# A rotation of three weight buffers instead of two across the last two weight quads of a sparse layer and the first of the next

## The reference

```python
def hybrid_layer(x, norm_g, w_in, ..., w_branch, w_out):
    h = rmsnorm(x, norm_g)
    proj = h @ w_in
    ...
    for i, o in enumerate((o_nsa, o_pool, o_conv, o_fox)):
        branch = (o * jax.nn.silu(gates[:, :, i])) @ w_branch[i]
        term = jax.nn.sigmoid(merge[:, :, i]) * branch
        acc = term if acc is None else acc + term
    return x + acc @ w_out
```

## Time and profile before

| what | value |
|---|---|
| median of 3 runs | 2235.05 us (2233.2 to 2238.94) |
| profiled execution, own time | 2234.29 us |
| its span in the profile | 2231.6 us |
| PE busy | 2156.6 us, 97% |
| DVE, ACT, POOL busy | 51%, 45%, 36% |
| mean granted PE clock | 0.995 |
| DMA | 189.32 MB, mean 85 GB/s |

### The profile page before, as it was taken

The page is one execution under the profiler, slowest core; times in us unless marked ns, Lnnn a source line. Parts: engine busy times, 40 slices in busy tenths (PEclk is TensorE's granted clock), DMA queues, the critical chain, the costliest instruction groups (busy, mean ns, idle before and its releaser), DMA issues.

```text
span 2231.6 us, 31209 instructions
## 1 busy us (share of the span) xinstructions
PE 2156.6 (97%) x11281; PEld 1772.5 (79%) x11281; DVE 1132.0 (51%) x2003; ACT 1004.3 (45%) x1950; POOL 794.7 (36%) x347
## 2 busy tenths in 40 slices
PE   5999999999989999999999999999999999999998
PEld 4788888788887888888887887777777787777776
DVE  5799999565442457452436532222286623222374
ACT  5768787752343433222223434444633434444631
POOL 2511111444464134444443333332343433333342
PEclk9999999999999999999999999999999999999998
DMA  3212111423333122223322222222223222222221
GB/s 142 91 57 63 64 61 62 142 85 97 101 124 95 39 76 85 95 94 95 103 94 100 89 77 71 67 76 67 85 93 120 87 83 75 69 67 68 85 95 57
DMA packets 51732, 189.32 MB, mean 85 GB/s; under 512 B 6564, under 2 KB 7204, under 8 KB 51108
## 3 DMA queue, kind: packets, MB, share of 16 engines
q1 hardware_dynamic: 48096, 175.13, 24.4%
q10 hardware_dynamic: 2452, 6.88, 0.8%
q0 software_dynamic: 1072, 5.77, 0.7%
HBM read 185.66 MB, written 2.10 MB: 84 GB/s over the span
## 4 chain that ended last, share of the span: by engine, by line
PE 78%; DVE 10%; ACT 4%; DVEq 3%; issue 2%; POOL 2%; DMA 0%; ACTq 0%; POOLq 0%
PE bank L350 21%; PE bank L352 20%; PE bank L351 20%; PE bank L951 2%; PE bank L994 2%; POOL weight_lo L382 1%; PE bank L977 1%; DVE wide_region L2264 1%; ACT wide_region L1078 1%; DVE wide_region L2267 1%; ACT weight_hi L376 1%; PE bank L425 1%; PE bank L609 1%; PE bank L915 1%; PE bank L830 1%
## 5 line engine op out<-in xcount | busy, mean ns | idle before, releaser
L382 POOL TENSOR_TENSOR weight_lo<-weight_slots,weight_hi 128x1024 fp32r<-128x1024 f32 x277 | 676.4, 2442 | 1020.5 <-ACT weight_hi L376 1015.1
L376 ACT ACTIVATE weight_hi<-weight_slots 128x1024 fp32r<-128x1024 f32 x272 | 288.0, 1059 | 778.5 <-PE bank L352 694.3
L350 PE MATMUL bank<-h_hi,weight_hi 128*128 128x512 f32 x1144 | 461.5, 403 | 2.3 <-issue 1.0
L351 PE MATMUL bank<-h_lo,weight_hi 128*128 128x512 f32 x1144 | 446.1, 390 | 0.0
L352 PE MATMUL bank<-h_hi,weight_lo 128*128 128x512 f32 x1136 | 443.5, 390 | 0.0
L350 PEld LDWEIGHTS bank<-h_hi,weight_hi 128*128 128x128 f32 x1144 | 214.8, 188 | 49.8 <-issue 3.1
L352 PEld LDWEIGHTS bank<-h_hi,weight_lo 128*128 128x128 f32 x1136 | 213.2, 188 | 45.8
L351 PEld LDWEIGHTS bank<-h_lo,weight_hi 128*128 128x128 f32 x1144 | 215.2, 188 | 40.5 <-issue 0.5
L382 POOL TENSOR_TENSOR head_weight_lo<-weight_slots,head_weight_hi 128x1024 fp32r<-128x1024 f32 x28 | 67.3, 2406 | 280.4 <-DVE v_region L1728 133.0
L350 PE MATMUL bank<-h_hi,head_weight_hi 128*128 128x512 f32 x336 | 139.2, 414 | 5.4 <-DVE h_lo L399 2.8
L2233 DVE RECIPROCAL small<-small 128x1 f32<-128x1 f32 x128 | 20.5, 160 | 230.2 <-ACT attention_work L1521 230.2
(11 more groups left out here) (491 smaller groups left out, 4484.4 us busy)
## 6 DMA issues: line engine op xcount, KB each, us to landing
weight_slots<-weights SPq DMA_DIRECT2D x328, 512.0 KB, 3.4
wide_region<-cmp_w ACTq DMA_DIRECT2D x2, 2048.0 KB, 8.6
v_region<-ssm_bc POOLq DMA_DIRECT2D x8, 256.0 KB, 4.4
residual<-x_in POOLq DMA_DIRECT2D x1, 2048.0 KB, 9.0
out<-normed SPq DMA_DIRECT2D x4, 512.0 KB, 2.7
residual<-x_in SPq DMA_DIRECT2D x2, 512.0 KB, 5.1
residual<-x_in ACTq DMA_DIRECT2D x2, 512.0 KB, 9.8
v_region<-mem_in POOLq DMA_DIRECT2D x1, 1024.0 KB, 5.1
```

Of the source, the lines that this page charges most:

```text
L350: pe.matmul(to, w_h[:, k, :], hi[:, k, 0:width], start=(k == 0), stop=False)
L351: pe.matmul(to, w_h[:, k, :], lo[:, k, 0:width], start=False, stop=False)
L376: act.activation(parts[0][s % 2], slot[s], ACT.Copy).then_inc(w_hi[s], 1)
L382: eng.tensor_tensor(parts[1][at], slot[s], parts[0][at].bitcast(F32), ALU.subtract).then_inc(w_lo[s], 1)
```

## The change

The buffers main 0, side, main 1 are used in turn for 12 blocks: those of quads `q0 + 17` and `q0 + 18` and, behind layer 0, those of the first quad of layer 1 (`W_TURN`). The text numbers these blocks n = 0 to 11. Block n may now be split when PE has finished block n - 3. Layer 1's last two quads take part as well, without a next layer. The loop over `ob` now splits blocks n = 1, 0 and 2 at its last two turns, n = 1 without any wait for PE; POOL takes n = 1 before n = 0 too. The first quad of sparse layer 0 stays as it was.

```diff
+        W_TURN = [[[W_MAIN[n][0], W_NEXT[n][1], W_MAIN[n][1]][(4 * q + i) % 3] for i in range(4)]
+                  for q in range(3) for n in range(2)]
+        W_TURN = [W_TURN[2 * q:2 * q + 2] for q in range(3)]
...
+                parts = W_TURN[2] if L else W_NEXT
...
-                both(pe, q0 + 17, ACC_HI, ACC_LO, SL * L + (S_L2 + S_ACC))
+                for i in range(2):
+                    for s in range(4):
+                        gemm(pe, q0 + 17 + i, s, ACC_HI, ACC_LO, T, SL * L + (S_L2 + S_ACC) if i + s == 0 else None,
+                             parts=W_TURN[i])
...
+            def turn_weight_hi(quad, n):
+
+                s, last = n % 4, n - 3
+                act.wait_ge(w_full[s], 16 * (quad + n // 4) + 16)
+                if last >= 0:
+                    act.wait_ge(mm_done[last % 4], quad + last // 4 + 1)
+                elif s != 1:
+                    act.wait_ge(mm_done[2 if s == 0 else 3], quad)
+                act.activation(W_TURN[n // 4][0][s], slot[s], ACT.Copy).then_inc(w_hi[s], 1)
...
-                next_weight_hi(q0, 3)
+                if L == 0:
+                    next_weight_hi(q0, 3)
+                else:
+                    turn_weight_hi(q0 - 2, 11)
...
                 for ob in range(KT + 1):
-                    if ob < KT:
+                    if ob < KT - 2:
                         ahead(act, q0 + (15 + ob // 4), ob % 4)
+                    elif ob == KT - 2:
+                        turn_weight_hi(q0 + 17, 1)
+                        turn_weight_hi(q0 + 17, 0)
+                    elif ob == KT - 1:
+                        turn_weight_hi(q0 + 17, 2)
                     if ob:
                         round_hi(act, stages + S_ACC, ob - 1, ACC_HI[:, ob - 1, :], ACC[:, ob - 1, :])
                 act.wait_ge(ms_ready, L + 8)
                 for blk in range(KT):
                     s, quad = blk % 4, q0 + (17 + blk // 4)
-                    if blk < KT - 2:
-                        ahead(act, quad, s)
-                    elif blk == KT - 1 and L + 1 < LAYERS:
-                        next_weight_hi(q0 + QL, 1)
-                        next_weight_hi(q0 + QL, 0)
+                    if blk + 3 < KT or L + 1 < LAYERS:
+                        turn_weight_hi(q0 + 17, blk + 3)
...
-                if L + 1 < LAYERS:
-                    next_weight_hi(q0 + QL, 2)
...
-                with pool.Fori(0, QL - 1) as i:
+                with pool.Fori(0, QL - 3) as i:
                     quad = pool.snap(i + (q0 + 1))
                     for s in range(4):
                         weight_lo(pool, quad, s)
+                for s in (1, 0, 2, 3):
+                    weight_lo(pool, q0 + 17, s, W_TURN[0])
+                for s in range(4):
+                    weight_lo(pool, q0 + 18, s, W_TURN[1])
```

More of the change, by code:

```diff
@@ L826, in _, with scaled_terms @@
             idle_products(pe, 18)
-            def scaled_terms(s, k):
-                w_h, w_l = W_NEXT[0][s], W_NEXT[1][s]
+            def scaled_terms(s, k, parts):
+                w_h, w_l = parts[0][s], parts[1][s]
                 pe.matmul(bank[s][:, :], w_h[:, k, :], T_HI[:, k, :], start=(k == 0), stop=False)
@@ L846, in _ @@
                         for s in range(2):
-                            scaled_terms(s, k)
+                            scaled_terms(s, k, parts)
                         pe.wait_ge(sq_ready, 7 * KT + (k + 1))
@@ L856, in _ @@
                             norm_sums(pe, L + 7, L + 6)
-                        scaled_terms(0, k)
+                        scaled_terms(0, k, parts)
                     pe.wait_ge(w_lo[1], q0 + 1)
@@ L861, in _ @@
                             norm_spread(pe, L + 7)
-                        scaled_terms(1, k)
+                        scaled_terms(1, k, parts)
                 pe.wait_ge(w_lo[2], q0 + 1)
@@ L866, in _ @@
                         norm_spread(pe, L + 7)
-                    scaled_terms(2, k)
+                    scaled_terms(2, k, parts)
                 pe.wait_ge(w_lo[3], q0 + 1)
                 for k in range(KT):
-                    scaled_terms(3, k)
+                    scaled_terms(3, k, parts)
                 if L:
@@ L2397, in _ @@
                 q0 = QL * L + Q_L2
-                weight_lo(pool, q0, 1, W_NEXT)
-                weight_lo(pool, q0, 0, W_NEXT)
                 if L == 0:
+                    weight_lo(pool, q0, 1, W_NEXT)
+                    weight_lo(pool, q0, 0, W_NEXT)
                     norm_power(pool, 6)
                     pool.wait_ge(rstd_ready, 7)
-                weight_lo(pool, q0, 2, W_NEXT)
+                    weight_lo(pool, q0, 2, W_NEXT)
+                else:
+                    for s in range(3):
+                        weight_lo(pool, q0, s, W_TURN[2])
                 norm_power(pool, L + 7)
                 pool.wait_ge(rstd_ready, L + 8)
-                weight_lo(pool, q0, 3, W_NEXT)
-                with pool.Fori(0, QL - 1) as i:
+                weight_lo(pool, q0, 3, W_TURN[2] if L else W_NEXT)
+                with pool.Fori(0, QL - 3) as i:
                     quad = pool.snap(i + (q0 + 1))
```

## The result

The changed kernel takes 2244.81 us (median of 7 runs, 2242.2 to 2246.47), the kernel before 2236.92 us beside it (7 runs). The ratio is 1.0036 with an interval of 1.0025 to 1.0047: slower by some 8 us. The forecast of 2241.9 us for a change of +6.8 us had the sign and most of the size. The prediction gave 0.49 each to slower and to the same by a line of 0.3%; the measured 0.36% lies just above it, so that it fell on the slower side of that line is not something the prediction foresaw. The profiled execution took 2244.25 us, 10.0 us more than the one of before.

What follows compares the result with a forecast made beforehand. PE, busy 97% of the span, was taken as the bound, with DVE at its limit in the merging loop. Terms: -4.5 + 9.8 + 1.5 = +6.8 us, forecast 2241.9 us, range 2232.5 to 2246.

Steps and rivals of the forecast that it cites:

- The steady part costs and gains nothing: Quads q0 + 17 and q0 + 18: weights are ready well ahead of PE with two buffers already; costed at nothing.
- -1.8 us, the bank next in line: Layer 1's start: PE's 2.57 us wait for POOL shrinks until DVE's residual addition of block 7 holds it; -1.8 us.
- -1.7 us, the clock at layer 1's start: Behind that shortened wait, the 3.4 us stretch at 1.2 GHz goes and 2.4 GHz stays; -1.7 us, the upper end.
- -1.0 us before the first `h_hi` product: At 1732.39 in layer 1: n = 11 split earlier, weights ready some 2 us earlier; -1.0 us, between 0 and 1.0.
- +4.9 us a layer in the merging loop: POOL's early subtractions hold off DVE's on-chip instructions, so low part 6 reaches PE late; +4.9 us per layer, bounds 0 to 7.2.
- All signs that were announced: Merging loop: POOL subtractions 3.5 and 3 us, two DVE instructions 2.9 each, PE waits 2.1 before `acc`, 4.3 before low part 6.
- +1.5 us for the clock in layer 0: Layer 0, behind PE's wait of some 4.3 us before low part 6: an added low-clock stretch; +1.5 us, between 0 and 1.7.
- a rival: More low clock: waits of 2.3 and 4.3 us per layer leave further 1.2 GHz stretches; +10 us, 2245 us; chance 0.14.
- DVE keeps the ports over back-to-back instructions: Merging loop: POOL cannot get in between, low part 6 only +1.1 us per layer; sum -2.3, 2232.8 us; chance 0.13.
- the early subtraction costs nothing: Merging loop: POOL's subtraction is late or DVE is ahead, so only the gains remain; -4.5 us, 2230.6 us; chance 0.12.
- The sum: Whole kernel: the terms make +6.8 us against the profiled execution's 2234.3 us, so 2241.1; forecast median 2241.9 us.

Runs made afterwards that it cites:

- POOL's other order: Changed kernel with ACT's list untouched, but POOL takes n = 0 before n = 1, in both layers: 2242.47 us, ratio 1.0036 to the kernel before.
- the late split: Changed kernel, three buffers kept, but n = 1 split only after the last branch block, n = 2 after the merging loop, POOL n = 0 first: 2232.68 us, ratio 0.9993.
- the late split in layer 0 alone: Changed kernel with the early split undone in layer 0 only, layer 1 as in the change: 2239.05 us, ratio 1.0017 to the kernel before.
- the swap with the new address: Kernel before, two buffers, n = 8 split and subtracted ahead of n = 9, side buffer 32 bytes further on: 2235.02 us, ratio 1.0005.
- the aligned late split: Changed kernel with its early split undone and 32 bytes of padding ahead of the side buffer: 2231.59 us, ratio 0.9986; measured again 2230.98 us, 0.9983.

## Why the prediction was right, point by point

- **The steady part costs and gains nothing.** Almost so. The blocks n = 1, 4, 7 of both layers and n = 10 are now on the side buffer, in place of 9 and 11. Five more blocks of 24 at 0.006 us are +0.7 us. This term is missing from the prediction. It stands in the rests of the account, 0.4 us for the three blocks of each layer and -0.15 for one block less at layer 1's start.
- **-1.8 us, the bank next in line.** 2.57 became 0.83 us, -1.74.
- **-1.7 us, the clock at layer 1's start.** The stretch is gone in the profile, and in none of the seven other executions in which PE stood still for only 0.8 us there did the clock fall. But behind the wait of 2.4 to 2.6 us it fell in only three of four profiles, so the term is worth 1.3 us on average, and the full 1.7 was partly the luck of the one profile that was read.
- **-1.0 us before the first `h_hi` product.** Gone, and by the mechanism named: ACT begins with the `h` blocks 0.8 us after DVE's first `normed` instead of 3.0, since n = 11 is split before them, and DVE's first `h_lo` takes 0.68 us instead of 2.54, since POOL is through. POOL's low part for the product is there 2.4 us before PE; it came 0.9 us after PE had stopped. That is 3.3 us earlier relative to PE, where the prediction had some 2. The three gains made -4.63 against -4.5.
- **+4.9 us a layer in the merging loop.** Counted from the first branch product, PE goes on with low part 6 5.03 us later in layer 0 and 5.05 in layer 1. All signs that were announced came: 3.39 for the 3.5 us and 2.85 for the 3 us on POOL, 2.73 and 2.88 on DVE, 1.97 before the first `acc` product for 2.1, 4.11 before low part 6 for 4.3. The one wait that I had not named is the 0.46 us before low part 5 in layer 1. The early subtraction is tested from both sides: without it the cost is gone, and alone in the kernel before it makes the cost.
- **+1.5 us for the clock in layer 0.** It fell behind low part 6 as forecast, 1.7 us. That the profile of before had no such stretch in layer 0 and one in layer 1 was chance, as the last section shows; over both layers the term is the same. It fell behind the 1.97 us wait as well, which I had given to a rival, and that cost nothing, since PE then waited for DVE anyway. In layer 1 the clock stayed up behind the 1.97.
- **The rivals.** That DVE keeps the ports over back-to-back instructions is out by L402's 2.88 us; that the early subtraction costs nothing, by the 4.11. The rule that the Trainium skill, SBUF — State Buffer, section "SBUF: two separate sides", states, that the first to start has the ports to its end, is borne out by these rows; what it leaves open, who is next, came out as taken from the earlier trace rows: the engine that has waited, not the one whose next instruction is already there.
- **The sum.** +6.8 against +7.5 in the regions and +7.9 in medians. Of the 0.7 us between the first two, 0.3 are the merging loops (5.03 and 5.05 for 4.9), 0.2 the clock of layer 0 and 0.2 the rests of the account. With the wait at layer 1's start followed by low clock in three cases of four, the account's +7.5 becomes some +8 on average, an estimate that agrees with the medians.

Still open is the clock's share over many runs. The mean granted clock is 0.9921 over the change's 7 runs and 0.9920 over the 5 with POOL's other order, but 0.9943 over 22 runs of the kernel before and 0.9944 over the 11 of the late split. The difference of 0.0022 is 4.9 us of full clock in 2240, where the account has one more stretch at half the clock on balance, 1.7 us. A profile shows one execution only, so how much of the 7.9 us is clock in the mean was not settled, nor why the late split in layer 0 alone lay some 3 us above what its profile adds up to (+1.0 us from layer 0's first branch product on).

## What to carry to other kernels

Moving a split, copy or cast to an earlier place is free only where no engine that shares its ports is full in that turn: here two POOL subtractions of 2.4 us beside short DVE instructions with both operands on chip cost DVE 2.0 and 2.2 us, and a third 1.1 us, and nearly all of it arrived at PE. Take the early work where DVE waits, and keep the rotation for the place that needs it. Compare the step between matmuls buffer by buffer: 6 ns a step from 32 bytes of address came to 33 us where the main buffers were moved, more than all the waits looked at here.

## What the runs showed of the hardware

- **The address of the weights.** Matmuls of 128x512 whose weights lie 32 bytes past a multiple of 64 follow each other every 0.233 us instead of 0.227 to 0.228, with either set of buffers in either place. What in the chip does this, no run tells.
- **A wait of 2 us is a toss for the clock.** In kernels whose merging loop is undisturbed PE waits 1.9 to 2.1 us for low part 6 in each layer. Nine profiles show 17 such waits; behind 8 of them the clock fell to 1.2 GHz for 3.4 us, behind 9 it did not, with the same matmuls ahead. One execution of the swap with the new address shows it behind layer 0's wait and not behind layer 1's:

```profile
1663.50:1666.90 3.40, 3.40 (x10) 2.63 (x9) 0.75 (x2) 1.36 (x2) 0.22 (x1) 0.53 0.04 7
2177.00:2180.40 3.40, 3.38 (x14) 2.64 (x15) 1.38 (x2) 1.53 (x3) 0.37 (x1) 1.00 0.16 66
```

and one of the aligned late split has full clock behind layer 0's wait and half behind layer 1's:

```profile
1659.90:1663.30 3.40, 3.31 (x14) 2.56 (x15) 1.42 (x3) 2.48 (x4) 2.27 (x1) 1.00 0.24 92
2171.50:2174.90 3.40, 3.40 (x9) 2.63 (x8) 0.69 (x1) 1.58 (x2) 3.40 (x2) 0.50 0.13 12
```

At the waits of 3.3 and 4.1 us it fell in all seven cases (in the two layers of the kernel with POOL's other order for 6.8 us, beginning 1.6 and 2.7 us before the wait's end), behind the one of 2.4 to 2.6 us at layer 1's start in three of four, behind the one of 0.8 us there in none of eight. So in this kernel a wait of 2 us is to be priced at its length and half of 1.7 us, and one of 4 us at its length and 1.7 or more; both are estimates from these few cases.
